# Attention of two small layers by pairs of heads on the halves of the matmul array, with two gate products moved behind the last pair

## The reference

```
u = layer_norm(x) * (1 + sc1) + sh1
(p_in, c_b, c_c, c_h, mq, mk, mv, fq, fk, fv, f_logit, gate_logit) = split(u @ w_in + b_in)
y_pool, y_conv = pool_mixer(p_in), conv_mixer(c_b, c_c, c_h)      # 256 columns each
y_moba = softmax(q_m k_m^T / 8 + causal mask) v                   # 4 heads of 64
y_fox  = softmax(q_f k_f^T / 8 + cum_q - cum_k + causal mask) v   # 4 heads of 64
merged = sum over n of sigmoid(gate_n) * (branch_n @ w_branch[n]) # n = pool, conv, moba, fox
x = layer_norm(ALPHA * x + g1 * (merged @ w_o)) ...               # then a feed-forward half
```

## Time and profile before

| what | value |
|---|---|
| median of 3 executions | 2495.14 us (2492.59 to 2495.36) |
| the profiled execution, its own time | 2496.76 us |
| its span, first to last instruction | 2494.7 us |
| mean granted clock of TensorE | 0.981 of full speed |
| TensorE busy | 93% of the span |
| VectorE / ScalarE busy | 41% / 14% |
| DMA | 701 MB, mean 281 GB/s |
| attention of layer 0, first scores to gate product 16 | 117.7 to 211.2 us |
| attention of layer 1, the same | 645.2 to 741.1 us |

### The profile page before, as it was taken

One profiled execution on the slowest core, in us unless ns is written; L12 is line 12 of the kernel. 1 busy time (PEld: TensorE's weight loads), 2 busy tenths in 40 slices (PEclk: granted clock), 3 DMA queues, 4 the chain that ended last, 5 costly groups with the idle time before them and its releaser, 6 DMA issues.

```text
span 2494.7 us, 26053 instructions
## 1 busy us (share of the span) xinstructions
PE 2325.5 (93%) x10320; PEld 1374.8 (55%) x10320; DVE 1022.3 (41%) x2216; ACT 353.7 (14%) x717; POOL 31.5 (1%) x54
## 2 busy tenths in 40 slices
PE   6999999999899999999998998898899989989986
PEld 5878688458678686467554333333377533333332
DVE  4254656756655567223744111111245621111113
ACT  1211111001121110011442111111100021111111
POOL 0100000001000000000000000000000000000000
PEclk9999999999899999999998999999999989999999
DMA  8644868856257688532046999999874369999996
GB/s 309 253 154 177 305 241 303 306 183 219 85 203 269 229 309 305 202 135 85 31 154 242 423 429 428 428 428 429 341 268 169 118 240 430 428 428 429 428 429 266
DMA packets 160899, 700.96 MB, mean 281 GB/s; under 512 B 6064, under 2 KB 15536, under 8 KB 135216
## 3 DMA queue, kind: packets, MB, share of 16 engines
q1 hardware_dynamic: 158512, 691.42, 70.3%
q0 software_dynamic: 2304, 8.39, 1.0%
HBM read 694.55 MB, written 5.24 MB: 281 GB/s over the span
## 4 chain that ended last, share of the span: by engine, by line
PE 72%; DMA 20%; DVE 5%; ACT 2%; issue 1%; SPq 1%; DVEq 0%; ACTq 0%
PE banks L616 71%; DMA ring<-in_exp_w_down_dram 19%; DVE acc L1788 1%; DMA ring<-in_w_ada_dram 1%; ACT UT L1406 1%; PE banks L749 0%; PE banks L681 0%; DVE acc L1761 0%; ACT arena L1613 0%; SPq L2581 0%; DVE arena L2206 0%; DVE arena L2213 0%; PE banks L1155 0%; DVE X L1863 0%; PE banks L996 0%
## 5 line engine op out<-in xcount | busy, mean ns | idle before, releaser
L616 PE MATMUL banks<-ring,arena 128*64 128x512 f32 (+2 forms) x3776 | 974.8, 592 | 80.8 <-DVE arena L2213 29.1
L616 PE MATMUL banks<-UT,ring 128*128 128x256 f32 (+1 forms) x3568 | 726.1, 363 | 6.0 <-ACT UT L1406 3.0
L616 PEld LDWEIGHTS banks<-ring,arena 128*64 128x64 f32 (+1 forms) x3776 | 360.8, 147 | 659.1 <-issue 617.6
L616 PEld LDWEIGHTS banks<-UT,ring 128*128 128x128 f32 x3568 | 618.7, 192 | 88.1 <-issue 15.3
L1788 DVE SCALAR_TENSOR_TENSOR acc<-ring,cact,acc 128x512 f32<-128x512 f32 x280 | 212.7, 760 | 9.9
L2205 DVE TENSOR_TENSOR arena<-arena,banks 128x512 f32<-128x512 f32 x32 | 34.0, 1062 | 441.1 <-PE banks L616 441.1
L1586 ACT ACTIVATE arena<-banks 128x512 f32<-128x512 f32 (+1 forms) x96 | 65.2, 679 | 798.2 <-PE banks L616 759.1
L616 PE MATMUL banks<-arena 64*128 64x512 f32 (+5 forms) x768 | 151.5, 444 | 5.0 <-ACT arena L1453 2.8
L616 PEld LDWEIGHTS banks<-arena 64*128 64x128 f32 (+2 forms) x768 | 74.0, 176 | 83.7 <-issue 68.6
L2213 DVE TENSOR_TENSOR arena<-banks,acc 128x512 f32<-128x512 f32 x32 | 22.1, 692 | 208.8 <-PE banks L616 208.8
L616 PE MATMUL banks<-ring,XN 128*128 128x512 f32 (+1 forms) x192 | 73.4, 542 | 0.0
(11 more groups left out here) (246 smaller groups left out, 1450.3 us busy)
## 6 DMA issues: line engine op xcount, KB each, us to landing
ring<-in_exp_w_gate_dram SPq DMA_DIRECT2D x64, 2048.0 KB, 22.1
ring<-in_exp_w_up_dram SPq DMA_DIRECT2D x64, 2048.0 KB, 25.2
ring<-in_exp_w_down_dram SPq DMA_DIRECT2D x64, 2048.0 KB, 17.1
ring<-in_w_in_dram SPq DMA_DIRECT2D x26, 2048.0 KB, 14.1
ring<-in_mod_w_dram SPq DMA_DIRECT2D x24, 2048.0 KB, 9.0
ring<-in_w_ada_dram SPq DMA_DIRECT2D x20, 2048.0 KB, 7.8
ring<-in_w_up_dram SPq DMA_DIRECT2D x16, 2048.0 KB, 9.8
ring<-in_w_down_dram SPq DMA_DIRECT2D x16, 2048.0 KB, 8.9
```

The lines of the kernel that those rows point to most:

```text
L616: return nc.tensor.matmul(o, lhs, rhs, start=start, stop=stop)
```

## The change

It reorders the 16 units of a layer so that two neighbours are the two heads of one pair (r = 0 and 1) with the same kind and the same block i: one on the first 64 rows or columns of the array, one on the second. The work is then laid out in turns p = 0 to 8. TensorE does in turn p:

1. the scores of both heads of pair p, one after the other into two banks (`head_scores`); in turn 8, where no pair is left, it waits there for the copy of `("o", l, 0, 0)`;
2. gate product 2p;
3. the transposes of both heads of pair p-1 (`head_turn`);
4. gate product 2p+1;
5. the value matmuls of pair p-1, the two heads taking turns (`head_weigh`).

So gate products 16 and 17 lie in turn 8, and the plain run begins with 18. ScalarE does in turn p both exponentials, gate 2p, both copies of pair p-1, gate 2p+1; the copy of the first attention's output (`head_out(l, 0)`) is moved to the start of turn 8, that of the second behind turn 8. VectorE does both maxima, gate product 2p-1, two operations of conditioning, both divisions, gate product 2p, two operations of conditioning. No arithmetic, no DMA and no matmul is added or removed; the order of the ring is as it was.

```diff
-                    for h in range(4):
-                        b = (h % 2) * HD
-                        for i in range(TT):
+                    for h2, i, r in itertools.product(range(2), range(TT), range(2)):
+                            h, b = 2 * h2 + r, r * HD
...
 # TensorE
-            def attention(L, extra=None):
...
+            def head_scores(two):
+                held = [take(pe, ("s",) + u["name"]) for u in two]
+                for bank, u in zip(held, two):
+                    x = mm(bank[:, 0:u["nk"]], u["q"], u["keys"][0][1], True, True)
+                    finish(x, ("s",) + u["name"])
+            def head_turn(l, two):
+                for u in two:
+                    g = ("t",) + u["name"]
+                    bank = take(pe, g)
+                    pe.wait_ge(prob_ready, UNIT_BASE[l] + u["n"] + 1)
+                    for k in range(u["nk"] // P):
+                        x = nc.tensor.transpose(bank[:, k * P:k * P + P], P1[:, u["n"] % 4, k * P:k * P + P], C("ident"))
+                    finish(x, g)
+            def head_weigh(l, two):
...
+                for u in two:
+                    wait_evicted(pe, ("t",) + u["name"])
+                for t in range(len(two[0]["values"])):
+                    for u in two:
+                        p0, p1, col = u["at"]
+                        x = mm(bank[p0:p1, col:col + P], u["values"][t], PT1[:, u["n"] % 2, t * P:t * P + P],
+                               t == 0, t == len(u["values"]) - 1)
+                if two[1]["last"]:
+                    finish(x, ("o", l, two[1]["name"][1], two[1]["hold"]))
+            def attention(l):
+                two = head_pairs(l)
+                for p in range(HEAD_PAIRS + 1):
+                    if p < HEAD_PAIRS:
+                        head_scores(two[p])
+                    else:
+                        wait_evicted(pe, ("o", l, 0, 0))
+                    gated_branch(l, 2 * p)
+                    if p:
+                        head_turn(l, two[p - 1])
+                    gated_branch(l, 2 * p + 1)
+                    if p:
+                        head_weigh(l, two[p - 1])
...
-                attention(l, lambda s: gated_branch(l, s))
-                for i in range(16, 32):
+                attention(l)
+                for i in range(18, 32):
                     gated_branch(l, i)
 # ScalarE
+            def attention(l):
+                two = head_pairs(l)
+                for p in range(HEAD_PAIRS + 1):
+                    if p < HEAD_PAIRS:
+                        for u in two[p]:
+                            col = UNIT_BASE[l] + u["n"]
+                            act.wait_ge(max_ready, col + 1)
+                            A(P1[:, u["n"] % 4, 0:u["nk"]], SM1[:, u["n"] % 2, 0:u["nk"]], ACT.Exp,
+                              bias=smax[:, col:col + 1], accum_out=ssum[:, col:col + 1]).then_inc(exp_ready, 1)
+                    else:
+                        head_out(l, 0)
+                    gate(l, 2 * p)
+                    if p:
+                        for u in two[p - 1]:
+                            g = ("t",) + u["name"]
+                            emptied(A(PT1[:, u["n"] % 2, 0:u["nk"]], filled(act, g)[:, 0:u["nk"]], ACT.Copy), g)
+                    gate(l, 2 * p + 1)
+                head_out(l, 1)
 # VectorE
+            def attention(l):
+                two = head_pairs(l)
+                for p in range(HEAD_PAIRS):
+                    for u in two[p]:
+                        head_largest(u)
+                    if p:
+                        gated_branch(l, 2 * p - 1)
+                    mod_part(MOD_SLOTS["in", l, 5 + p // 2], 2 * (p % 2))
+                    for u in two[p]:
+                        head_probabilities(u)
+                    gated_branch(l, 2 * p)
+                    mod_part(MOD_SLOTS["in", l, 5 + p // 2], 2 * (p % 2) + 1)
+                gated_branch(l, 15)
+                mod_evict(MOD_SLOTS["in", l, 8])
```

More of the change, by code:

```diff
@@ L579, in pairs, with head_pairs @@
             return [us[2 * p:2 * p + 2] for p in range(PAIRS)]
+        def head_pairs(l):
+            us = numbered(l)
+            return [us[2 * p:2 * p + 2] for p in range(HEAD_PAIRS)]
         def turns(p, two):
@@ L728, in wview @@
                 return piece(pe, key)[:, 0:8 * cols].rearrange("p (k n) -> p k n", n=cols)
-            def attention(L, extra=None):
[L731 to L756, removed]
-                        p0, p1, col = u["at"]
[L758 to L765, removed]
@@ new lines, in head_weigh @@
+            def head_weigh(l, two):
+                if two[0]["first"]:
+                    take(pe, ("o", l, two[0]["name"][1], two[0]["hold"]), two[0]["hold"])
+                bank = banks[:, BANKS + two[0]["hold"], :]
+                for u in two:
+                    wait_evicted(pe, ("t",) + u["name"])
+                for t in range(len(two[0]["values"])):
+                    for u in two:
+                        p0, p1, col = u["at"]
+                        x = mm(bank[p0:p1, col:col + P], u["values"][t], PT1[:, u["n"] % 2, t * P:t * P + P],
+                               t == 0, t == len(u["values"]) - 1)
+                if two[1]["last"]:
+                    finish(x, ("o", l, two[1]["name"][1], two[1]["hold"]))
@@ L1453, in copied @@
                 emptied(A(dst, filled(act, g), ACT.Copy), g)
[L1455 to L1475, removed]
@@ new lines, in head_out @@
+            def head_out(l, m):
+                g = ("o", l, m, m)
+                bank = filled(act, g)
+                bv = S(f"bin{l}")[:, 12 + 6 * m:14 + 6 * m]
+                for c in range(2):
+                    x = A(Y[:, 4 + 2 * m + c, :], bank[:, c * N:c * N + N], ACT.Identity, bias=bv[:, c:c + 1])
+                emptied(x, g)
+            def attention(l):
[16 more added lines that the diff above has]
+                head_out(l, 1)
@@ L1924, in _ @@
             roped = [0]
[L1926 to L1946, removed]
-                    if s:
-                        u = us[s - 1]
-                        n, nk, g = u["n"], u["nk"], ("s",) + u["name"]
-                        c = UNIT_BASE[L] + n
-                        total = ssum[:, c:c + 1]
-                        dve.wait_ge(exp_ready, c + 1)
-                        if u["sink"] is not None:
-                            link(V.tensor_tensor(total, total, ssink[:, c:c + 1], ALU.add))
-                        x = V.reciprocal(total, total)
-                        if u["mask"] is None:
-                            emptied(x, g)
-                            wait_evicted(dve, g)
-                        else:
-                            link(x)
-                        p = pr[:, prob_slot(L, u), 0:nk]
-                        V.tensor_scalar(p, p, total, None, ALU.mult).then_inc(prob_ready, 1)
-                    if extra is not None:
-                        extra(s)
@@ new lines, in head_largest @@
+            def head_largest(u):
+                n, nk, g = u["n"], u["nk"], ("s",) + u["name"]
+                c = UNIT_BASE[u["name"][0]] + n
+                col = smax[:, c:c + 1]
+                emptied(V.tensor_tensor_reduce(out=SM1[:, n % 2, 0:nk], in0=filled(dve, g)[:, 0:nk], in1=u["mask"],
+                                               scale=1.0, scalar=-3e38, op0=ALU.add, op1=ALU.max, accum_out=col), g)
+                wait_evicted(dve, g)
+                V.tensor_scalar(col, col, -1.0, None, ALU.mult).then_inc(max_ready, 1)
```

17 lines of the change are left out of this document (9 added, 8 removed).

## The result

| | before | changed |
|---|---|---|
| median | 2495.02 us (6 runs) | 2473.89 us (6 runs, 2473.38 to 2475.72) |
| ratio | 1 | 0.9919, 95% interval 0.9907 to 0.9932 |
| profiled execution | 2496.76 us | 2475.72 us |
| its span | 2494.7 us | 2473.8 us |

The change saves 21.1 us between the medians; the ratio puts it at 0.81%. Forecast were 19.1 us. The first view is the timeline of TensorE over two turns of layer 0's attention in the changed kernel. It answers to the earlier trace rows.

A forecast was written before the change was run, and what follows sets the result against it. TensorE's own queue was taken to bound both attentions. New pieces summed to 92.60 us a layer against 102.16, saving 9.56, twice 19.1; from the 2495.1 us median that gives 2476.0 us, own range 2470 to 2483, wider range 2468 to 2487.

The forecast's parts named there:

- What bounds the stage: In both layers' attentions TensorE is busy all of the time, so only shortening its own queue counts.
- The overlap of halves: In score and value pairs, two heads on opposite array halves run at once, saving 0.64 us per pair.
- score pairs of 128 columns: Scores of two heads over 128 keys: 0.42 us with full overlap, 0.62 with none; 0.42 taken.
- Fewer changes of form: In each turn the array switches less often between whole and half-array modes, saving 0.72 us per pair.
- the gate product ahead of values: On TensorE in turns 1 to 8, the gate product followed by value matmuls takes 4.52 us.
- small conditioning products: Four small matmuls of the conditioning in a layer's attention, about 0.2 us each, 0.80 us in all.
- wait of turn 8: Before gate product 16 TensorE stands about 0.72 us for ScalarE's copy of the first attention's output; bounds 0 to 1.3.
- The thin place: Gate product 10 needs gate product 8's bank, behind late conditioning on VectorE; covered by 0.9 us, 2 us more costs 1.1.
- The gain reaches the end: Both layers' savings of 9.56 us count, 19.1 in all; rival, lost at a later join, chance 0.05.
- The 11.5 us wait in layer 1: TensorE waits for VectorE before layer 1's attention; VectorE's chain was forecast to move earlier with layer 0.
- The clock: Rival: TensorE's clock falls to its lower level, 1.2 GHz, and the time ends above 2495 us; chance 0.04.
- tail: Drained stretch before gate product 16 in the old order, 2.6 us, of which about half was called work.

The follow-up runs named there:

- pairs on the same half: Changed kernel with each pair made of heads on the same array half, values one head after the other; 2482.66 us, ratio 0.9943 to the kernel before.
- second run of the changed kernel: The changed kernel run once more with no edit; 2473.83 us, ratio 0.9911 to the kernel before.
- values not beside scores: Changed kernel with transposes right behind the scores and values between the two gate products of a turn; 2480.72 us, ratio 0.9943 to the kernel before.
- early copy: Changed kernel with ScalarE's copy of the first attention's output in turn 6 instead of turn 8; 2471.59 us, ratio 0.9903 to the kernel before.
- values apart: Changed kernel with a pair's value matmuls one head after the other, heads still on different halves; 2474.85 us, ratio 0.9918 to the kernel before.

## Why the prediction was right

**What bounds the stage.** Right. TensorE is busy for 70.85 of 70.85 us of layer 0's turns, and for 71.01 of 71.45 in layer 1, where the 0.44 us are the wait before gate product 10.

**The overlap of halves**, 0.64 us a turn: right, 0.645 by the pairs on the same half. It holds for score pairs of 128 columns too, which no row of before had: in the second run of the changed kernel the first such pair takes 116.61 - 116.18 = 0.43 us, forecast 0.42; on the same half it takes 117.66 - 117.02 = 0.64.

**Fewer changes of form.** Right in kind, too small in size. Forecast 0.72 us a turn; measured 11.64 - 21.62 / 2 = 0.83, from the turns of the run on the same half, which has the new order and no overlap. The mis-sized term is the gate product ahead of values, taken at 4.52 us. It takes 4.41. The 4.52 of the earlier trace rows belonged to a gate product that had half-array pieces on both sides, and I read all of its 0.21 us as the side ahead. One side costs 0.1, as the row of 4.52 in the run with values not beside scores confirms. In 8 turns and 2 layers that is 16 x 0.11 = 1.8 us of the 2.6 us by which the two stages' gain, 21.7 us (worked out below), passed the forecast of 19.1. The medians show 21.1, and that this stands nearer to the forecast is chance. The small conditioning products cost 0.13 us each (0.22 from start to start, and 0.09 less for the gate product ahead, which takes 4.32), not 0.20, and layer 0 has three of them up to gate product 18, not four: 0.4 us instead of 0.80 there, 0.5 in layer 1, which has four. The wait of turn 8 is 0.84 us, not 0.72. From the modelled end of gate product 15 to the start of 16 pass 199.15 - 197.81 = 1.34 us, forecast 1.30; but TensorE's own work covers 0.50 of it, not 0.58, because I counted that work from the start of the next row and ScalarE's from the modelled end.

Could each small piece simply have a fixed price, whatever its form? Then fewer and longer pieces would save as much without any change of form. The transposes speak against it: two of them between gate products take 132.08 - 131.86 = 0.22 us, which is what they stream, while between two half-array pieces of the old order they took 0.37. The direct step from values to scores isn't cheaper than another: four values and four scores of 128 columns take 0.79 us, forecast 0.38 + 0.42.

From first scores to gate product 18 the changed kernel, where no clock disturbed it, took 207.61 - 116.18 = 91.43 us; forecast 92.60. The kernel before took 219.97 - 117.70 = 102.27, forecast from its parts 102.16.

**The wait in turn 8.** Right, with its cause; the early copy removed it.

**The thin place.** Named rightly, and the price of a longer transfer too; its cover was put at 0.9 us and is 0.7. Where the piece takes 7.9 us from issue to first use, or 8.1 at the most, TensorE stands for nothing. In layer 1 it took 9.03 in the changed kernel's profile (wait 0.44), 9.35 with the early copy (0.76) and 9.39 with values apart (0.79). All three give 8.6 us as the longest that is covered. Why this transfer takes 7.9 us in one execution and 9.4 in another isn't known.

**The gain reaches the end.** Right. The 11.5 us wait in layer 1 is unchanged, and the two stages' gains, 102.27 - 91.43 = 10.8 us and (749.85 - 645.17) - (729.78 - 635.97) = 10.9 us, add up to 21.7 (layer 0 from the changed kernel's second run, layer 1 from its first), of which 21.1 show in the medians.

**The clock.** The rival didn't come: 1.00 in the turns of both layers. In the changed kernel's profile the lower clock at gate product 0 of layer 0 cost 5.24 - 3.55 = 1.7 us against its next run; that is ahead of the attention's first transposes, so they didn't cause it; what did isn't known. At gate product 0 of layer 1 it is low in both kernels, behind the wait of 11.5 us (0.51 from 640 to 650 us before, 0.51 from 630 to 640 in the changed kernel). The Trainium skill ("TensorE: Matmul & The Clock Gate", Part 4: PE-mode transpose) says that transposes don't count as busy for the gate in the same way as other work. Four of them in a row, 0.44 us, did no harm here; no run here tests a longer row.

## What to carry to other kernels

When small matmuls that fill half the array lie between big ones, put those that use opposite halves next to each other, and arrange the work so that the array changes its form less often. Each of the two was worth some 5 us a layer here, and they add. The second came mostly from doing pieces of one form two heads at a time (eight changes for two units became three); that values and scores are neighbours is only 1.2 us of it. Before crediting a tail or a cover, look at what the stretch holds besides work; 2.6 us of "tail" held 0.4 us of idle time. When an operation is moved behind another in an engine's queue, look for a bank given back inside it.

## What the runs showed of the hardware that was not expected

The two heads' value matmuls overlap fully whether they alternate or come head by head: twelve instructions take 1.22 and 1.23 us. The Trainium skill ("TensorE: Matmul & The Clock Gate", Part 3: Packing small matmuls) says that matmuls start and end strictly in program order; by that a group of eight in head order would take 0.21 us more, one of the two cases of the expectation. The measurement decides: on two column halves in float32 strict order doesn't hold for the starts. In the trace of the run with values apart, the eight value instructions start two by two, at 146.90 and 146.92, 147.06 and 147.08, 147.17 and 147.19, 147.28 and 147.30 us, though the program gives one head's four first. With both heads on the same half they start one by one, 0.11 us apart.

A change between whole array and half array costs on both of its sides. The gate product beside it takes 0.1 us more (4.31, 4.41, 4.52 us with none, one and two such neighbours), and the half-array piece itself 0.15 to 0.2.
